# Two projections of the same input in a Trainium2 kernel: one sum of squares for both, and the second's first weight panel split inside the stage between them

## What is computed

```python
hn = rmsnorm(h, norm_mix[l])             # x * rsqrt(mean(x * x) + eps) * gain
h = h + even_mixer(hn, even_w_in[j], ...)

def even_mixer(h, w_in, gn_gain, w_out, rel_bias, n_keep):
    p = h @ w_in
    aq, ak, av, iq, ik, iw, bq, bk, bv, bg = jnp.split(p, splits, axis=-1)
    a_out = dsa_attention(aq, ak, av, iq, ik, iw * (IDX_HEADS ** -0.5), rel_bias, n_keep)
    r = retention(rotary(bq), rotary(bk), bv)
    r = group_norm(r) * gn_gain          # written out in the reference
    r_out = r * jax.nn.silu(bg)
    return jnp.concatenate([a_out, r_out], axis=-1) @ w_out
```

## Time and profile before

| | |
|---|---|
| time, median of 3 runs | 2411.99 us (2411.28 to 2412.50) |
| the profiled execution's own time | 2409.96 us |
| its span, first to last instruction | 2408.2 us |
| PE busy | 2280.4 us, 95% |
| PE weight load, beside PE | 2113.8 us, 88% |
| DVE busy | 1112.1 us, 46% |
| ACT busy | 989.8 us, 41% |
| POOL busy | 670.6 us, 28% |
| mean granted TensorE clock | 0.974 |

### The profile page before, as it was taken

How to read it: one execution, slowest core, us unless ns; L and a number is a source line. 1 busy time by engine, 2 the same in 40 slices (tenths; PEclk the granted TensorE clock), 3 DMA queues, 4 the chain that set the end, 5 groups by cost and what they waited for, 6 DMA issues and landing times. The chain is left out here.

```text
span 2408.2 us, 39806 instructions
## 1 busy us (share of the span) xinstructions
PE 2280.4 (95%) x16936; PEld 2113.8 (88%) x16936; DVE 1112.1 (46%) x1623; ACT 989.8 (41%) x1452; POOL 670.6 (28%) x515
## 2 busy tenths in 40 slices
PE   7998898998898998898999999999999989999999
PEld 6996588995588997797699999999889879999998
DVE  2446634437624214587644433444555544433443
ACT  5327543337544334533633322334555533322322
POOL 2003223003223704435522311322333312320321
PEclk9999999999999998998999999999999999999999
DMA  5323022220022220222033324323111113324322
GB/s 184 119 88 98 5 71 70 86 84 4 2 70 76 71 71 27 71 66 93 2 96 102 86 73 112 94 73 95 53 46 43 36 36 90 103 74 112 88 78 72
DMA packets 235231, 175.90 MB, mean 73 GB/s; under 512 B 7732, under 2 KB 230060, under 8 KB 234544
## 3 DMA queue, kind: packets, MB, share of 16 engines
q1 hardware_dynamic: 235056, 173.37, 23.9%
HBM read 171.20 MB, written 10.09 MB: 75 GB/s over the span
## 5 line engine op out<-in xcount | busy, mean ns | idle before, releaser
L327 DVE TENSOR_TENSOR panel_lo<-panel_raw,panel_hi 128x2048 fp32r<-128x2048 f32 (+2 forms) x150 | 336.9, 2246 | 301.1 <-ACT panel_hi L319 301.1
L319 ACT ACTIVATE panel_hi<-panel_raw 128x2048 fp32r<-128x2048 f32 (+2 forms) x155 | 275.9, 1780 | 390.5 <-PE product L408 259.7
L408 PE MATMUL product<-scaled_hi,panel_hi 128*128 128x264 f32 (+2 forms) x1408 | 285.4, 284 | 2.6 <-PEq L464 1.4
L408 PE MATMUL product<-scaled_lo,panel_hi 128*128 128x264 f32 (+2 forms) x1408 | 284.3, 283 | 0.0
L408 PE MATMUL product<-scaled_hi,panel_lo 128*128 128x264 f32 (+2 forms) x1408 | 282.7, 282 | 0.0
L421 PE MATMUL product_banks<-panel_hi,scaled_hi 128*128 128x256 f32 x912 | 258.7, 284 | 5.4 <-DVE scaled_lo L3773 4.7
L421 PE MATMUL product_banks<-panel_hi,scaled_lo 128*128 128x256 f32 x912 | 257.5, 282 | 0.0
L421 PE MATMUL product_banks<-panel_lo,scaled_hi 128*128 128x256 f32 x912 | 257.3, 282 | 0.0
L408 PEld LDWEIGHTS product<-scaled_hi,panel_hi 128*128 128x128 f32 x1408 | 217.1, 189 | 3.0 <-issue 3.0
L408 PEld LDWEIGHTS product<-scaled_lo,panel_hi 128*128 128x128 f32 x1408 | 218.0, 188 | 0.0
L408 PEld LDWEIGHTS product<-scaled_hi,panel_lo 128*128 128x128 f32 x1408 | 217.7, 189 | 0.0
(11 more groups left out here) (488 smaller groups left out, 5348.3 us busy)
## 6 DMA issues: line engine op xcount, KB each, us to landing
panel_raw<-in_w_in_dram SPq DMA_DIRECT2D x26, 1024.0 KB, 5.4
panel_raw<-in_ffn_w_gate_dram SPq DMA_DIRECT2D x44, 512.0 KB, 4.0
panel_raw<-in_ffn_w_up_dram SPq DMA_DIRECT2D x44, 512.0 KB, 5.2
panel_raw<-in_ffn_w_down_dram SPq DMA_DIRECT2D x32, 704.0 KB, 4.7
panel_raw<-in_even_w_in_dram SPq DMA_DIRECT2D x21, 1024.0 KB, 5.1
panel_raw<-in_odd_w_in_dram SPq DMA_DIRECT2D x12, 1024.0 KB, 5.1
panel_raw<-in_w_out_dram SPq DMA_DIRECT2D x8, 1024.0 KB, 5.1
panel_raw<-in_even_w_out_dram SPq DMA_DIRECT2D x8, 768.0 KB, 4.8
```

What stands on the lines that cost most here:

```text
L319: act.activation(c.hi[g % 2][:, 0:used], c.raw[g % 2][:, 0:used], ACT.Copy).then_inc(c.hi_made.sem, 1)
L327: dve.tensor_tensor(c.lo[g % 2][:, 0:used], c.raw[g % 2][:, 0:used], c.hi[g % 2][:, 0:used].bitcast(F32), ALU.subtract).then_inc(c.lo_made ...
L408: done = pe.matmul(to, weight(w, k), a[:, k, u:v], start=(k == 0 and x == 0), stop=(k == chunks - 1 and x == 2))
```

## The change

The sum of squares of the first product is kept in a buffer of its own (`even_total`) and used again by the second, which makes no squares and no additions, and has PE's sums over the partitions one tile earlier (tile 1, same step). The second product's first panel is split within the retention, on ACT's and DVE's lists behind the first head's work; the retention's eight tables stand in the two panel buffers of the other parity, three in each, and two in new tiles.

```diff
@@ led_product_stage
-        norm = Rstd(c, stage, ..., squares=..., whole=True, spread=wide)
+        norm = Rstd(c, stage, ..., squares=..., total=total, whole=True, spread=wide,
+                    summed=summed)
...
-                for k in range(KD):
-                    norm.act_square(act, k)
-                    if k == 1:
-                        panels.hi(act, first + 1)
+                if summed:
+                    panels.hi(act, first + 1)
+                else:
+                    for k in range(KD):
+                        norm.act_square(act, k)
+                        if k == 1:
+                            panels.hi(act, first + 1)
                 norm.act_inverse(act, sums, columns)
...
-                for k in range(KD):
-                    norm.pool_add(pool, k)
+                if not summed:
+                    for k in range(KD):
+                        norm.pool_add(pool, k)
...
-                        if wide and at == (2 if own else 3):
+                        if wide and at == (1 if summed else 2 if own else 3):
                             between = lambda slot: norm.pe_sums(pe, sums, columns) if slot == (SUMS_SLOT_OWN if own else 0) else None
@@ retention_stage
-        slot = [t[:, PAD * n:PAD * (n + 1)] for t in (*c.hi, *c.lo) for n in range(2)]
+        used = 1 - next_panel % 2
+        slot = [t[:, PAD * n:PAD * (n + 1)] for t in (c.hi[used], c.lo[used]) for n in range(3)]
+        slot += [c.sb(f"ret_slot{n}", [P, PAD], F32R, into=stage)[:] for n in range(2)]
...
+                    if i == 0:
+                        c.panels.hi(act, next_panel)
...
+                    if i == 0:
+                        c.panels.lo(dve, next_panel)
@@ even_layer
+        total = c.sb("even_total", [P, NB2 * P], side="right", into=norm)[:]
...
-            led_product_stage(c, retention, ..., RotarySide(c, cell.rows, shared), opened=True)
-            retention_stage(c, cell.rows, y)
+            led_product_stage(c, retention, ..., RotarySide(c, cell.rows, shared), opened=True, total=total)
+            retention_stage(c, cell.rows, y, selected.first)
...
-                    led_product_stage(c, selected, ..., IndexSide(...))
+                    led_product_stage(c, selected, ..., IndexSide(...), opened=True,
+                                      total=total, summed=True)
+                norm.close()
@@ Rstd.pe_sums
-                pe.wait_ge(c.sum_added.sem, c.sum_added.at(self.adds))
+                pe.wait_ge(c.sum_added.sem, c.sum_added.at(0 if self.summed else self.adds))
```

More of the change, by code:

```diff
@@ L551, with led_product_stage @@
 SUMS_SLOT_OWN = 6
-def led_product_stage(c, product, src, tokens, gain, split, update=None, side=None, opened=False):
+def led_product_stage(c, product, src, tokens, gain, split, update=None, side=None, opened=False, total=None, summed=False):
     nc, panels = c.nc, c.panels
@@ L595, in last_tail @@
             return max((n for n in range(at) if is_tail(n)), default=-1)
-        norm = Rstd(c, stage, lambda k: src[:, k, :], tokens, squares=side.room_for_squares() if side is not None else None, whole=True, spread=wide)
+        norm = Rstd(c, stage, lambda k: src[:, k, :], tokens, squares=side.room_for_squares() if side is not None else None, total=total, whole=True, spread=wide,
+                    summed=summed)
         parts = Parts(c, stage, src, tokens, gain, room=whole)
@@ L2885, in close, with retention_stage @@
         self.c.rope_part.base += 6 * NB2
-def retention_stage(c, rows, y):
+def retention_stage(c, rows, y, next_panel):
     nc = c.nc
@@ L3117, in even_layer @@
         y = shared[:].rearrange("p (b n) -> p b n", b=NB2)
+        norm = ExitStack()
+        total = c.sb("even_total", [P, NB2 * P], side="right", into=norm)[:]
         with ExitStack() as half:
             cell.rows = c.sb("rows", [P, NB2, 3072], into=half)
-            led_product_stage(c, retention, c.hT, TOK, 4, split, update, RotarySide(c, cell.rows, shared), opened=True)
-            retention_stage(c, cell.rows, y)
+            led_product_stage(c, retention, c.hT, TOK, 4, split, update, RotarySide(c, cell.rows, shared), opened=True, total=total)
+            retention_stage(c, cell.rows, y, selected.first)
         with ExitStack() as half:
@@ L3132, in even_layer @@
                     cell.iw = c.sb("iw", [P, NB2, 8], side="right", into=index)
-                    led_product_stage(c, selected, c.hT, TOK, 4, split, None, IndexSide(c, index, cell, score, best, spare))
+                    led_product_stage(c, selected, c.hT, TOK, 4, split, None, IndexSide(c, index, cell, score, best, spare), opened=True,
+                                      total=total, summed=True)
+                norm.close()
                 sliding = c.sb("sliding_bias", [P, A2_HEADS, WIDE2], into=attention)
@@ L3753, in close @@
         c = self.c
-        for counter, n in ((c.squared, KD), (c.sum_added, self.adds), (c.sums_ready, 1), (c.root_made, 1), (c.rstd_ready, 1)):
+        squares = () if self.summed else ((c.squared, KD), (c.sum_added, self.adds))
+        for counter, n in (*squares, (c.sums_ready, 1), (c.root_made, 1), (c.rstd_ready, 1)):
             counter.base += n
```

3 lines of the change are left out of this document (2 added, 1 removed).

## The result

| | before | after |
|---|---|---|
| median | 2411.99 us (3 runs, 2411.28 to 2412.50) | 2396.21 us (3 runs, 2395.18 to 2398.98) |
| profiled execution's own time | 2409.96 us | 2395.18 us |
| its span | 2408.2 us | 2393.4 us |
| mean granted clock | 0.974 | 0.979 |

The ratio on record is 0.9948, with a 95% interval of 0.9933 to 0.9962, which is 12.5 us of 2412; the medians themselves stand at 0.9935, 15.8 us apart, near the interval's lower end. The changed kernel is faster, by less than 1%.

A forecast was written before the change was run, and what follows sets the result against it. PE, busy 95% of the span, was taken as the bound, with gains only where it waits or runs at low clock. Terms 1.45 + 1.09 + 2.19 + 0.63 + 2.63 gave 8.0 us: 2412.0 to 2404.0, range 2401.5 to 2407.2.

The forecast's parts named there:

- first tile and tile 0: Second product's opening: first tile held only by PE's stream, gaining 1.45 us; tile 0 in 5.86 not 6.95, gaining 1.09.
- The wait for POOL: Second product, in front of PE's sums: with no additions left to wait for, 2.19 us goes.
- The 18 steps: Second product, tile 2's steps behind the sums: clock stays at 1.00, so 7.03 us shrinks to 4.40, gaining 2.63.
- The sums one tile earlier: Second product: sums cost tile 1 what they no longer cost tile 2; third panel still ready in time, no wait.
- The wait at the first score: Tile 4, first score of the index: PE's wait grows from 2.49 to about 2.9 us, chain before it unchanged.
- The retention: Splitting the second product's first panel there costs 0, within DVE's cover of 0.3 us and PE's of 1.3.
- The collision with POOL's gate weighting: Retention: the moved low part might meet POOL's weighting, 0.2 us apart; DVE would wait 0.7 us, cost still 0.
- (a): Rival: clock falls behind the sums in their new place; 2.63 us stay, gain 5.4, 2406.6 us. Chance 0.10.
- (b): Longer wait at tile 4 moves the low clock; gain 6.5 to 9.4 us, width of the likeliest case, no separate chance.
- (d): Rival: at the opening PE is held by something unseen, its instruction queue; only the sums' 5.4 us comes. Chance 0.05.
- (e): Rival: split stops PE in the retention and the clock stays low until the second product; +12 us, 2424. Chance 0.02.
- (c): Rival: the retention doesn't hide the split; PE loses up to 4.2 us there, gain 3.8, 2408.2 us. Chance 0.06.

The follow-up runs named there:

- before_again: The kernel before the change, unedited, profiled and timed a second time; ratio 1.0 (0.9991 to 1.0008), mean 2409.4 us.
- before_filled: The kernel before, with two useless streamed products added ahead of PE's sums to fill its wait for POOL; ratio 1.0, mean 2408.4 us.
- late_sums: The changed kernel with PE's sums over the partitions put back in tile 2; ratio 0.997, mean 2402.3 us against 2408.4 before.
- after_third: The changed kernel, unedited, run a third time; ratio 0.9971, mean 2401.6 us against 2408.2 for the kernel before.
- short_stream: The changed kernel with one useless product, not four, streamed ahead of the second product's first tile; ratio 0.9954, mean 2397.3 us.
- after_again: The changed kernel, unedited, run a second time; ratio 0.9956, mean 2399.6 us against 2409.1 for the kernel before.
- after_padded: The changed kernel with nine more useless products in the second product's opening stream, 13 in place of 4; ratio 1.0006, mean 2409.4 us.

## Why the prediction came out as it did

**The opening, right in its sum.** Predicted were 8.0 us at tile 2's end, 23.4 us behind the stream's start; it is 23.27, and 8.05 us at the keys. The terms, from the changed kernel's rows: tile 1 starts 9.36 us behind the stream's start, 12.05 before, which makes 2.69 for the two terms of first tile and tile 0 (2.54 predicted). Within them the first tile starts sooner than the modelled end of the stream let expect, at 3.11 us and not 3.6, and tile 0 takes 6.25 us and not 5.86. The wait for POOL, 2.19: the sums start 969.83 - 968.36 = 1.47 us into tile 1 as predicted. The sums take 2.11 us (969.83 to 971.94), 0.63 as predicted. The 18 steps take 976.42 - 971.94 = 4.48 us where 4.40 were written: 2.55 for 2.63. All terms together: 8.06.

**What the terms hide.** The working sorted the loss of before by the waits of one execution. It left out a second wait for `scaled_lo`, 0.76 us inside tile 0, which is most of the 1.09 us that it took off there. In the other way through the opening (before_again) there is no wait for POOL; PE waits 0.77 and 0.81 us inside tile 0, and the third panel costs 2.78. The total is the same, since the chain of squares, additions, sums, inverse root and third panel stands behind both. That the sum could be made from one execution was therefore right for the sum and not for the names of its terms.

The term of 2.63 us for the clock in the 18 steps has the wrong name above all. From the sums' start to tile 3 it is 9.53 us wherever the clock stayed up (before_again, before_filled, late_sums), with a wait for the third panel at its end, and 10.15 us in the profile of before. The difference, 0.62 us, is what the sums alone lost (2.74 us in place of 2.11). At the higher clock PE would have finished the 18 steps 2.63 us sooner and would then have waited for the panel. The term came true because the sums moved one tile up, so that the panel was there in time.

**The sums one tile earlier, right that nothing waits, and not priced.** The prediction derived that the third panel comes in time for tile 3. late_sums shows what that was worth, 2.6 us: with the sums in tile 2, the waits in front of them go and a wait of 2.78 us for `panel_lo` takes their place. The prediction took the move as a thing that costs nothing and did not see that it earns: these 2.6 us are its clock term under another name.

**The wait at the first score, right.** 2.92 us for 2.9, and the chain from the keys to the first score is 9.23 us (9.24 before).

**The retention, right but for 0.3 us.** The length shows no cost beyond 0.1 us at the clocks where a kernel without the split was seen. The collision with POOL's gate weighting was weighed with a distance of 0.2 us between the two, and the distance is one that varies. POOL's and DVE's rows of the changed kernel, and then of after_third:

```profile
907.02 7.61 POOL L3073 TENSOR_TENSOR rows<-rows,group_gain 128x256 f32<-128x256 f32 x11 [4.46 <-DMA group_gain<-in_even_gn_gain_dram]
...
913.96 2.81 DVE L327 TENSOR_TENSOR panel_lo<-panel_raw,panel_hi 128x2048 fp32r<-128x2048 f32 x1 [0.80 <-ACT panel_hi L319]
```

```profile
906.18 7.59 POOL L3073 TENSOR_TENSOR rows<-rows,group_gain 128x256 f32<-128x256 f32 x11 [4.32 <-DMA group_gain<-in_even_gn_gain_dram]
...
913.75 2.29 DVE L327 TENSOR_TENSOR panel_lo<-panel_raw,panel_hi 128x2048 fp32r<-128x2048 f32 x1 [0.80 <-ACT panel_hi L319]
```

In the first, POOL ends at 914.63, 0.67 us into the low part, and this takes 2.81 us. In the second, POOL ends at 913.77, at the low part's start, and it takes 2.29. The Trainium skill, SBUF — State Buffer, "Who interferes with whom", has DVE's second SBUF input and GpSimd's read take turns; both rows agree, and the price is 0.52 us on DVE. PE then waited 0.35 us for a decay in that execution, a wait that the prediction put at zero and named as a sign of being wrong:

```profile
917.45 0.39 PE L2947 MATMUL ret_scores<-panel_hi,panel_lo 128*128 128x272 f32 x1 [0.35 <-DVE decayed L3020]
```

short_stream has the same (low part 2.71 us, wait 0.24), also at a clock of 0.94. after_again met the same collision (2.76 us) at 0.91 and had no such wait of PE: the cover of 1.3 us was read where the clock was low, and at the higher one PE comes to the score sooner. The retention's length does not follow the wait; it goes with its granted clock, 58.33 us at 0.94, 59.52 and 59.55 at 0.89, 60.34 at 0.86.

**The rivals.** (a), a fall of the clock behind the sums in their new place, did not happen in any profile of the changed kernel. (b), the low clock moved at tile 4, happened in some executions of either kernel: the stretch from the first score to the ranking's end takes 76.4 or 77.8 us before, and 76.5 or 77.8 after. It is a draw and no property of the change. (d) and (e) did not occur, nor did (c) at its price of 4.2 us: the most that PE waited for the split was 0.35.

**The step that failed: "Its own range by (b) and by the spread of the runs (1.2 us) is 2402.2 to 2405.9."** Three runs within 1.2 us were taken for the spread of the kernel. Executions of the kernel before vary with a standard deviation of 2.4 us, by 10.9 us from the lowest to the highest; those of the changed kernel with 3.3. The anchor of 2412.0 is 3.3 us above the mean of the 68 later executions, and the changed kernel's 2396.2 is 3.8 below its mean of 15; with the 8.8 us between the means this makes up the 15.8 that were measured, by construction. Anchored at the mean, the forecast would read 2408.7 - 8.0 = 2400.7; the changed kernel takes 2400.0 on the mean, 2400.8 without its first three. The size of the change was right, and the range had no term for the largest uncertainty. It was a rare draw, if it was one: two means of three executions each, with these deviations, differ by chance by some 2.4 us (an estimate from 2.4 and 3.3), and the first two lie 7 us further apart than the later ones. Why both sets of the first result lay so far out, in opposite directions, is not shown.

**Could it be seen before?** Partly. The profile of before has stretches at the low clock outside of the opening, such as the one in the earlier trace rows at 905 to 915, and each is a stretch whose place another execution may draw anew. A range should have had a few microseconds for them on both sides. Its size could not be read from one trace.

What stays open: what decides how much of the first 900 us is at the low clock, and so whether the retention starts at 900 or at 905. The changed kernel shows both ends (900.7, 904.7 and 900.0); the kernel before showed only the later one (904.9 and 903.7, and 904.6 in before_filled). after_padded started its retention at 900.57 and was no faster than the kernel before on the mean, which speaks against a gain of the change there; no instruction there was changed but for the place of the sum.

## What to carry to other kernels

Price a change in distances between rows of one stage: here they repeated to 0.13 us while the whole time moved by nearly 11 us between executions, and a gain of 8 us read from them agreed with the later means when the medians of three runs said 15.8. Before you take back what a low clock cost, look at what else ends there: here 2.63 us of it hid a chain that would have held PE just as long. When a small gain in one stage comes with a larger one in the total, pad the stage by what it gained: if the total returns to that of before, nothing else was gained. When a producer is removed from the front of a chain (squares and additions in front of the sums), look at once at what the chain releases behind it: moving its consumer one tile earlier was worth 2.6 of the 8 us.

## What the runs showed of the hardware

**The granted clock's low stretches fall differently in each execution, and cost whole microseconds.** The changed kernel's retention, the same in nine of the profiles, took from 58.20 us at a clock of 0.94 (short_stream) to 60.92 at 0.86 (after_padded). In front of the retention the low clock cost from 22.2 us (after_third) to 27.3 (after_again) of one program. A like wait does not always bring it down: behind the wait of 2.9 us at the first score it stayed at 1.00 in the changed kernel's first profile and fell in after_again and after_third. Over all, one kernel's executions reached from 2402.3 to 2413.2 us. The Trainium skill, TensorE: Matmul & The Clock Gate, Part 1, says that the number of products run at the low clock varies from run to run, which agrees. It calls the cost of the ramp at a kernel's start less than 1% of a typical span; here the mean granted clock of 0.974 lies 2.6% under full speed, since the clock falls again and again within the kernel. The executions' times differ by up to 0.45%, more than the 8 us of this change, and the clock is a part of that.

**A collision between DVE and POOL goes with the course of a stage.** The eight `scaled_lo` took 5.52 us without POOL's additions, and 6.97 or 8.13 us beside them in two executions of one program. So the kernel before has two ways through its opening, with waits in different places and the same end to 0.13 us.
